# Expert outputs stored by index into token rows and read back with plain loads; the conformer layer norm in two token parts

## What is computed

```
def odd_mixer(h, ...):                       # layer 1
    z = h @ w_pw1 + b_pw1;  za, zg = split(z);  u = za * sigmoid(zg)
    c = causal_dwconv([ctx, u], dw_w) + dw_b             # 31 taps
    c = silu(layer_norm(c, ln_g, ln_b))
    return c @ w_pw2 + b_pw2

def hier_moe(h, ...):                        # both layers, x is (544, 1024)
    g_idx       = top 1 of softmax(x @ w_rg)             # 4 groups
    e_idx, e_w  = top 2 of the group's 8 experts         # 32 experts in all
    act = silu(x @ w_gate[e]) * (x @ w_up[e])            # width 256
    y   = sum over the token's two experts of e_w * (act @ w_down[e])

x = x + mixer(rms_norm(x));  x = x + hier_moe(rms_norm(x))    # each layer
y = rms_norm(x, g_final)
```

## Time and profile before

| | us |
|---|---|
| time, median of 3 runs | 1278.84 (1275.76 to 1280.82) |
| profiled execution | 1286.39 |
| its span, first to last instruction | 1284.6 |
| TensorE busy | 1098.6 (86%) |
| VectorE, ScalarE, GpSimd busy | 377.8, 225.7, 116.9 |
| mean granted TensorE clock | 0.930 |
| bytes moved | 304.78 MB |

### The profile page before, as it was taken

How to read it: one execution, slowest core, us unless ns; L and a number is a source line. 1 busy time by engine, 2 the same in 40 slices (tenths; PEclk the granted TensorE clock), 3 DMA queues, 4 the chain that set the end, 5 groups by cost and what they waited for, 6 DMA issues and landing times.

```text
span 1284.6 us, 18797 instructions
## 1 busy us (share of the span) xinstructions
PE 1098.6 (86%) x7117; PEld 688.4 (54%) x7118; DVE 377.8 (29%) x710; ACT 225.7 (18%) x402; POOL 116.9 (9%) x168
## 2 busy tenths in 40 slices
PE   5999998899869977787749999989969978898990
PEld 4887685676445434344328776754435544454440
DVE  2000012342251111111154899733261211111116
ACT  4000110344201101101141101134111111011112
POOL 1000000100010100000031211100001101111003
PEclk9999997899879989989879999999979999899995
DMA  9623024700467999999972110060095999999966
GB/s 379 268 92 144 30 85 70 292 1 9 160 249 273 412 412 411 413 411 412 393 242 79 67 66 1 16 238 21 33 376 199 412 402 396 402 350 394 412 233 233
DMA packets 79855, 304.78 MB, mean 237 GB/s; under 512 B 8416, under 2 KB 8448, under 8 KB 77600
## 3 DMA queue, kind: packets, MB, share of 16 engines
q1 hardware_dynamic: 54576, 242.76, 48.2%
q0 software_dynamic: 8784, 31.48, 6.9%
q10 hardware_dynamic: 16416, 29.45, 6.6%
HBM read 269.85 MB, written 33.83 MB: 236 GB/s over the span
## 4 chain that ended last, share of the span: by engine, by line
PE 51%; DMA 24%; DVE 11%; issue 9%; ACT 4%; POOLq 0%; POOL 0%; DVEq 0%; ACTq 0%; SPq 0%
DMA ring<-w_moe 15%; PE psum L1442 10%; DMA ar<-w_moe 7%; PE psum L1625 6%; PE psum L1548 6%; PE psum L1757 5%; DVE ar L1307 4%; PE psum L1436 3%; PE psum L1719 3%; PE psum L1680 2%; PE psum L1493 2%; PE psum L1653 2%; DVE X L1060 1%; PE psum L1509 1%; PE psum L1380 1%
## 5 line engine op out<-in xcount | busy, mean ns | idle before, releaser
L1625 PE MATMUL psum<-ring,ar 128*64 128x256 f32 x1408 | 180.0, 401 | 31.3 <-DMA ring<-w_moe 29.6
L1625 PEld LDWEIGHTS psum<-ring,ar 128*64 128x64 f32 x1408 | 102.0, 143 | 106.2 <-DMA ring<-w_moe 35.7
L1442 PE MATMUL psum<-ar,ring 128*128 128x272 f32 x576 | 132.7, 393 | 0.0
L1757 PE MATMUL psum<-ar,ring 128*128 128x272 f32 x512 | 120.8, 397 | 3.0 <-DVE ar L1293 3.0
L1442 PEld LDWEIGHTS psum<-ar,ring 128*128 128x128 f32 x576 | 109.3, 190 | 22.9 <-issue 0.3
L1757 PEld LDWEIGHTS psum<-ar,ring 128*128 128x128 f32 x512 | 97.8, 192 | 28.0 <-issue 4.2
L1307 DVE SCALAR_TENSOR_TENSOR ar<-ar,sv 128x512 f32<-128x512 f32 x120 | 107.0, 893 | 5.8 <-ACT ar L860 1.9
L1236 DVE COPY ar<-psum 128x128 f32<-128x128 f32 x64 | 18.7, 292 | 281.2 <-PE psum L1670 281.2
L1625 PE MATMUL psum<-ar 128*64 128x256 f32 x640 | 84.9, 409 | 18.6 <-DMA ar<-w_moe 18.6
L1680 PE MATMUL psum<-ring,ar 128*64 128x512 f32 x352 | 84.1, 598 | 0.8 <-DVE ar L1236 0.4
L1548 PE MATMUL psum<-ring,ar 128*128 128x512 f32 x192 | 84.1, 594 | 0.0
(11 more groups left out here) (209 smaller groups left out, 1154.4 us busy)
## 6 DMA issues: line engine op xcount, KB each, us to landing
ring<-w_moe SPq DMA_DIRECT2D x44, 3072.0 KB
ar<-w_moe SPq DMA_DIRECT2D x20, 3072.0 KB, 17.6
expert_outputs<-ar ACTq DMA_DIRECT2D x128, 128.0 KB
ring<-w_mix SPq DMA_DIRECT2D x4, 3072.0 KB, 13.6
ring<-w_pw SPq DMA_DIRECT2D x6, 2048.0 KB, 10.8
ring<-kv_in SPq DMA_DIRECT2D x2, 2880.0 KB, 11.6
expert_outputs<-ring POOLq DMA_DIRECT2D x8, 512.0 KB, 11.4
normed_rows<-ar ACTq DMA_DIRECT2D x8, 512.0 KB, 2.6
```

Of the source, the lines that this page charges most:

```text
L1442: t = mm(psum[:, b + h, 0:HALF], w[:, k, P * c:P * c + P], hT[:, k, HALF * h:HALF * h + HALF], start=k == 0, stop=k == KD - 1)
L1625: t = mm(psum[64 * f:64 * f + 64, u % 2, 0:2 * P], xt[:, k, 64 * (u % 2):64 * (u % 2) + 64], w[:, k, f, :], start=k == 0, stop=k == KD - 1)
L1757: t = mm(psum[:, b + h, 0:HALF], w[:, k, o:o + P], hT2[:, k, HALF * h:HALF * h + HALF], start=k == 0, stop=k == KD - 1)
```

## The change

- **Table.** C is now scaled with a code, 2 x token + which of its two experts, less 4096 (`C_CODE`), so that after doubling and adding 8192 and the half's number (`C_HALF`) `tb` holds for every job, row and half the row of `ys_dram` where it belongs, and a number past the end where the row is empty. `tg`, which is `tb` shifted right by two, is the token to gather. DVE has one instruction of 48 columns and three shifts where it had two copies.
- **Rows in.** The gathers of `xn_dram` have a bound and leave empty rows out. So that the buffers hold finite numbers, POOL clears the three `xg` and `xe` once in each layer; the last of the `xg` is cleared after the table is ready and ahead of the first gather.
- **Rows out.** ACT no longer stores. POOL copies a column of `tb` to `ixy` and issues one indirect DMA of 128 pieces x 2 KB into `ys_dram`, now 4 pieces for each token (two experts x two halves), and leaves the empty ones out. `ys_dram` has 2176 rows of 512. The writing of zeros at the start goes.
- **POOL's order.** For each expert u: gather a pair (u even), the rest of u's chunks with their outputs, the first chunk's rows of u+1, the output of u.
- **Combine.** SP waits for `all_out` and reads both outputs of each tile of tokens with one plain load (`fetch`, five loads, four of 1 MB). The last `w_pw1` blocks wait for the fourth.
- **Layer norm.** In two token parts, 256 to 543 first, then 0 to 255. The second part's squares are made on POOL. `project(3)` takes the tiles in the order 4, 2, 3, 0, 1; the second part's variance comes on PE after tile 4. The filler goes from 10 to 5 matmuls.

```diff
+LN_PART = ((256, TOK), (0, 256))
+PW2_ORDER = (4, 2, 3, 0, 1)
...
-        ys_dram = nc.dram_tensor("expert_outputs", ((EXPERTS + MORE) * JOB, D), F32, kind="Internal").ap()
+        ys_dram = nc.dram_tensor("expert_outputs", (4 * TOK, 512), F32, kind="Internal").ap()
...
+            def fetch(n):
+                sp.wait_ge(moe.all_out, n + 1)
+                for i in range(TILES):
+                    src = ys_dram.rearrange("(t q) c -> t (q c)", q=4)[P * i:P * i + ROWS[i], :]
+                    sp.dma_start(yg[i][0:ROWS[i], :], src).then_inc(moe.fetched[i], 16)
...
-            nc.gpsimd.memset(ring[:, 3, 0:D], 0.0).then_inc(zeros_made, 1)
...
-                pool.dma_start(ys_dram[o:o + P, :], ring[:, 3, 0:D]).then_inc(zeros_out, 16)
...
-                pool.wait_ge(moe.tokens, n + 1)
+                pool.dma_start(spare_dram, cst[0:JOB, C_FOLD:C_FOLD + 32]).then_inc(ex[n].out, 16)
+                pool.wait_ge(moe.places, n + 1)
+                nc.gpsimd.memset(xg[0], 0.0).then_inc(moe.rows_clear, 1)
                 pool.wait_ge(moe.jobs, n + 1)
+                nc.gpsimd.memset(xg[1], 0.0).then_inc(moe.rows_clear, 1)
+                pool.wait_ge(moe.tokens, 3 * n + 3)
+                nc.gpsimd.memset(xg[2], 0.0).then_inc(moe.rows_clear, 1)
...
+                    pool.indirect_dma_start(xg[v], None, xn_dram, bass.IndirectOffsetOnAxis(ixg[:, v:v + 1], 0),
+                                            bounds_check=TOK - 1, oob_is_err=False).then_inc(moe.rows_in[v], 16)
...
+                def chunk_out(chunk):
+                    pool.wait_ge(ex[n].kept, chunk + 2)
...
+                def further_rest(it, u):
+                    chunks, before = counts(it, u)
+                    with pool.If(chunks > 0):
+                        with pool.If(chunks > 1):
+                            with pool.Fori(1, chunks) as c:
+                                chunk_rows(before + c)
+                                chunk_out(before + c - 1)
+                        chunk_out(before + chunks - 1)
+
+                def outputs(it, u):
+                    b = u % 3
+                    pool.wait_ge(moe.y_kept, MSLOTS * it + (EXPERTS * n + u + 1))
+                    nc.gpsimd.tensor_copy(ixy[:, b:b + 1], tb[:, bass.ds(MSLOTS * it + u, 1)]).then_inc(moe.iy_ready, 1)
+                    pool.wait_ge(moe.iy_ready, MSLOTS * it + (EXPERTS * n + u + 1))
+                    pool.sem_inc(moe.seen, 1)
+                    pool.indirect_dma_start(ys_dram, bass.IndirectOffsetOnAxis(ixy[:, b:b + 1], 0), yj[b], None,
+                                            bounds_check=4 * TOK - 1, oob_is_err=False).then_inc(moe.y_out[b], 16)
+
+                def body(it, gathers, jobs=MSLOTS, last=False):
+                    for u in range(jobs):
+                        if u % 2 == 0 and gathers:
+                            rows_of(3 * it + (u // 2 + 4), u + 8)
+                        further_rest(it, u)
+                        if not (last and u == jobs - 1):
+                            further_first(it, u + 1)
+                        outputs(it, u)
...
-                pool.wait_ge(moe.all_out, n + 1)
-                for q in range(2 * TILES):
-                    i, k = q // 2, q % 2
-                    pool.indirect_dma_start(
-                        yg[q][0:ROWS[i], :], None, ys_dram,
-                        bass.IndirectOffsetOnAxis(ix[0:ROWS[i], i, k:k + 1], 0)).then_inc(moe.gathered[q], 16)
...
+            lo, hi = LN_PART[1]
+            for k in range(KD):
+                pool.wait_ge(centred, KD + k + 1)
+                nc.gpsimd.tensor_tensor(sq[:, k, lo:hi], cT[:, k, lo:hi], cT[:, k, lo:hi], ALU.mult
+                                        ).then_inc(squared_late, 1)
...
-                    act.wait_ge(moe.y_kept, MSLOTS * it + (EXPERTS * n + u + 1))
-                    store(MSLOTS * it + u, yj[b], moe.y_out[b])
...
+            variance(0)
+            stay_warm(5, 4)
             for c in range(2):
                 pe.wait_ge(later_w[c], 32)
-            project(3, cT, KD, lambda k, h: ring[:, PW1_SLOT[h], 512 * k:512 * k + 512], pw2_done)
+            project(3, cT, KD, lambda k, h: ring[:, PW1_SLOT[h], 512 * k:512 * k + 512], pw2_done,
+                    lambda: variance(1))
```

More of the change, by code:

```diff
@@ L275, in __init__ @@
                 self.y_out = [sem(f"y_out_{b}") for b in range(3)]
-                self.gathered = [sem(f"gathered_{q}") for q in range(2 * TILES)]
+                self.fetched = [sem(f"fetched_{i}") for i in range(TILES)]
                 self.all_out = sem("all_out")
@@ L489, in _ @@
             experts(1)
+            fetch(1)
             for i in range(TILES):
@@ new lines, in counts, with chunk_rows @@
+                def counts(it, u):
+                    return (pool.value_load(jt[0:1, bass.ds(MSLOTS * it + (EXPERTS * what + u), 1)],
+                                            min_val=0, max_val=MORE) for what in range(2))
+                def chunk_rows(chunk):
+                    pool.wait_ge(ex[n].turned, chunk + 1)
+                    o = nc.s_assert_within(chunk + MORE, MORE, 2 * MORE - 1,
+                                           skip_runtime_bounds_check_because="at most MORE chunks")
+                    nc.gpsimd.tensor_copy(ixe[0:JOB, 0:1], tg[0:JOB, bass.ds(o, 1)]).then_inc(ex[n].ix, 1)
+                    pool.wait_ge(ex[n].ix, chunk + 1)
+                    pool.sem_inc(moe.seen, 1)
+                    pool.indirect_dma_start(xe, None, xn_dram, bass.IndirectOffsetOnAxis(ixe[0:JOB, 0:1], 0),
+                                            bounds_check=TOK - 1, oob_is_err=False).then_inc(ex[n].rows, 16)
@@ new lines, in chunk_out @@
+                def chunk_out(chunk):
+                    pool.wait_ge(ex[n].kept, chunk + 2)
+                    o = nc.s_assert_within(chunk + EXPERTS, EXPERTS, JOBS - 1,
+                                           skip_runtime_bounds_check_because="at most MORE chunks")
+                    nc.gpsimd.tensor_copy(ixy[:, 3:4], tb[:, bass.ds(o, 1)]).then_inc(ex[n].iy, 1)
+                    pool.wait_ge(ex[n].iy, chunk + 1)
+                    pool.sem_inc(moe.seen, 1)
+                    pool.indirect_dma_start(ys_dram, bass.IndirectOffsetOnAxis(ixy[:, 3:4], 0), ye, None,
+                                            bounds_check=4 * TOK - 1, oob_is_err=False).then_inc(ex[n].out, 16)
@@ L770, in silu @@
                     nc.scalar.activation(sg, psum[:, u % 2, 0:P], ACT.Silu).then_inc(moe.sg_ready, 1)
-                def store(job, y, done):
-                    rows = ys_dram.rearrange("(j r) c -> j r c", r=JOB)[bass.ds(job, 1), :, :].rearrange(
-                        "a r c -> (a r) c")
-                    for q in range(2):
-                        act.dma_start(rows[:, 512 * q:512 * q + 512], y[64 * q:64 * q + 64, :]).then_inc(done, 16)
                 def keep_y(it, u, first):
@@ L804, in further @@
                             nc.scalar.activation(ye, psum[:, 6, :], ACT.Copy).then_inc(ex[n].kept, 1)
-                            act.wait_ge(ex[n].kept, before + c + 2)
-                            job = nc.s_assert_within(before + c + EXPERTS, EXPERTS, EXPERTS + MORE - 1,
-                                                     skip_runtime_bounds_check_because="at most MORE chunks")
-                            store(job, ye, ex[n].out)
                 def finish(it, u, first):
@@ L1735, in mean @@
                 wait_conv(pe, k)
[L1736 to L1738 removed]
+                for h, (lo, hi) in enumerate(LN_PART):
+                    t = mm(psum[:, h, 0:hi - lo], mean_of, cT[:, k, lo:hi], start=k == 0, stop=k == KD - 1)
                 return t
```

191 lines of the change are left out of this document (98 added, 93 removed).

## The result

The changed kernel takes 1291.05 us (median of 8 runs, 1287.59 to 1294.64), the kernel before 1281.82 beside it (8 runs). The ratio is 1.0072 with a 95% interval of 1.0049 to 1.0095: **slower by 0.7%**, where 1.5% faster was forecast. The profiled execution took 1288.67 us, its span 1286.9. What follows is read against before's profiled execution of 1286.39 (span 1284.6).

What follows compares the result with a forecast made beforehand. Layer 0's experts were taken as bound by weight loads, layer 1's mostly by PE. Terms -16.2 - 6.2 + 2.6 - 1.0 - 4.7 + 7.0 = -18.5 us gave 1260.3 us; 8-in-10 range 1250 to 1280.

Steps and rivals of the forecast that it cites:

- What bounds what: Layer 0's experts bound by weight loads on full DMA engines; layer 1's by PE from 1056.2 us on.
- rival b: GpSimd (POOL) sets the experts' pace if a scatter takes over 2.9 us; at 4 us, 1289 us; chance 0.08.
- Bytes in layer 0: Empty rows left out of gathers and stores free DMA time in layer 0's load-bound experts: -16.2 us.
- Bytes in layer 1: Empty rows left out save time only in layer 1's load-bound stretch, 986 to 1056 us: -6.2 us.
- Start: Before each layer's first gather, wider table, more DVE steps and buffer clearing, less a smaller gather: +1.3 us a layer.
- End: After each layer's experts, last scatter, then plain loads for the adds in place of gathers: -0.5 us a layer.
- Layer norm: Two token parts let PE start the second product's sample rows sooner, tile 2 at 869.1 for 873.8: -4.7 us.
- Chunks: In layer 1, rows for experts 15 and 23 wait behind the previous chunk's output, 3.4 us of PE each: +7 us.

Runs made afterwards that it cites:

- both: The changed kernel with GpSimd's expert loop written out and the next expert's first chunk gathered ahead of the next pair's rows and the last scatter: 1265.9 us, ratio 0.9848.
- shift: The changed kernel with 111 or 47 idle semaphore increments in GpSimd's program between the two layers' experts: 1285.79 us with 111, 1277.86 us with 47.
- move_all: both, but empty rows are gathered too and empty output rows stored behind the token rows: 1294.35 us, ratio 1.0111.
- straight: The changed kernel with only GpSimd's loop over the experts written out as straight code: 1277.84 us, ratio 0.9961.
- both_again: both, run once more unchanged: 1262.87 us, ratio 0.9863.

## Why the prediction was wrong

**What bounds what.** Right: layer 0 on the loads, layer 1 from expert 11 on PE. The prediction then asked for GpSimd only whether its work fits between PE's (rival b, decided at 2.9 us for a scatter). A scatter takes 0.99 us, as forecast, so (b) as written is out. What made GpSimd late was not the length of its steps but their order, and the stops at its loop's turn.

**Bytes in layer 0,** forecast -16.2: -15.2 in the changed kernel, -9.3 and -12.3 in the two traces of `both`. Right in the changed kernel, 4 to 7 us too large for `both`, of which some 3 go with the written-out loop. The pieces of the chain came down to about 17.0 us with a gather (16.6 to 17.8), not 16.4.

**Bytes in layer 1,** forecast -6.2 (its own factors give 6.1): 0 in the changed kernel's trace, but -2.0 and -2.4 in the two `shift` kernels, which have the same experts, and -2.6 in `both`, from expert 0 to 10. Undoing it (`move_all`) costs 4.8 there. Right in kind; the gain that came is less than half of it.

**Start,** forecast +1.3 a layer (the terms named add to 1.15): +2.0 in layer 0 and -0.2 in layer 1 from logits to first gate_up. Near in the sum, off in each. **End,** forecast -0.5: the seam behind layer 0's experts, from the end of the last `down` to the end of the last mean product, went from 207.6 to 206.2 us, the last one by -1.2. Right in kind; the scatter landed in 2.37 us in the empty queue.

**Layer norm,** forecast -4.7: -4.8 alone (interval +0.3 to -6.4, so not clear of nothing), -6.4 in the stretch in the changed kernel's trace. Right for the stretch; it moved nothing in the changed kernel's time.

**Chunks,** forecast +7 for two waits of 3.4 us: this is the step that failed. PE waits 35.6 us for chunks, five times. The two waits of the forecast are there, of 4.96 and 5.29, since rows of 7 and 4 tokens land in 6.14 and 6.52 us where 5.0 was taken. Three more are not in the prediction. Expert 11's (7.43) could have been read from the diff: `rows_of` waits for PE, and the next expert's chunk had been put behind it, where before a chunk's rows were fetched a whole expert earlier. I traced the queue behind `chunk_out` and not the one behind `rows_of`. Experts 14's and 22's (11.39 and 6.55) are for the most part made by the stops; without these, in `straight`, 3.31 and 2.30 are left. The profile of before had no such stop to read, but the order of GpSimd's program showed that the body of its loop had grown (from 123 instructions to 352), and the Trainium skill's page "Runtime: NRT & Kernel Launch", section "Instruction fetch mechanics", says that a taken branch out of the two pieces held waits for a DMA.

The sum missed 28.6 us of PE's time. That `both`, without these waits, comes out at 0.9848 and 0.9863, beside the forecast of 1260.3 (0.9855 of the 1278.84 it was made from), is luck in part. Set to the one wait of 1.7 us that `both` has, in place of the 7.0, the forecast is 1255.0 or 0.981. The measured ratios are 0.3 to 0.5% above that, 4 to 6 us, and the bytes' terms are too large there by more than as much.

**The range** ended at 1280 and should have held a case in which GpSimd is late for another cause than its load; rival (b) had the right time, 1289, and the wrong mechanism.

## What to carry to other kernels

When a change lengthens the program of an engine that loops, count the instructions of the body and look for packets on the instruction queue at each turn. If they come back, write the loop out or move it, before judging the change itself (here the stops were worth 8 to 13 us). Follow each gather that is moved back to every wait that now stands ahead of it, not only to the nearest. And an edit that gains in its own stretch and moves nothing in the total may be hidden by another edit's stall: measure it alone and with the stall removed.

## What the chip showed unexpectedly

A few waits of PE cost more than their length. The product of a chunk's rows (32 matmuls) takes 3.69 us at a granted clock of 1.00 in `both_again`; in `both`, behind a wait of the same 1.7 us, it took 6.30 at a granted clock of 0.58, so most of it at 1.2 GHz and not at 2.4. From the chains of waits, `both_again` and then `both`:

```profile
1082.55 3.69 PE psum L1718 x32
```

```profile
1086.84 6.30 PE psum L1718 x32
```

The same happened at expert 22 (3.67 against 6.59 us), and makes most of the 5.9 us between the two traces of one kernel in the stretch from expert 10 to 30. The landing time of a gather by index falls little with its filled rows where the loads fill the DMA engines: in the changed kernel 8.14 us for 64 rows, 6.73 for 41, 6.14 and 6.12 for 7, and 6.52 for 4. A scatter with the queue empty took 2.35 us.
